# The third weight slot split ahead of the norm's root in four stages, and the first state-space weights split in the stage ahead

## The reference, cut to what matters

```
def rmsnorm(x, g):
    xf = x.astype(jnp.float32)
    y = xf * lax.rsqrt(jnp.mean(xf * xf, axis=-1, keepdims=True) + EPS)
    return (y * g.astype(jnp.float32)).astype(x.dtype)
...
        h = rmsnorm(x, norm_mix[i])
        proj = h @ w_in[i]
...
        merged = (jax.nn.sigmoid(gate_a) * (attn @ w_attn_branch[i])
                  + jax.nn.sigmoid(gate_b) * (ssd @ w_ssd_branch[i]))
        x = x + merged @ w_out[i]
        h = rmsnorm(x, norm_cross[i])
        x = x + cross_attention(h, rmsnorm(mem, norm_mem[i]), w_xq[i], w_xkv[i], w_xo[i])
        h = rmsnorm(x, norm_ffn[i])
        x = x + jnp.square(jax.nn.relu(h @ w_up[i])) @ w_down[i]
```

## Time and profile before

| | |
|---|---|
| median of 3 runs | 2428.04 us (2426.35 to 2433.3) |
| span of the profiled execution, first to last instruction | 2430.9 us |
| busy share of the span | PE 92%, DVE 58%, ACT 44%, POOL 14% |
| mean granted TensorE clock | 0.960 |

### The profile page before, as it was taken

One profiled execution on the slowest core, in us unless ns is written; L12 is line 12 of the kernel. 1 busy time (PEld: TensorE's weight loads), 2 busy tenths in 40 slices (PEclk: granted clock), 3 DMA queues, 4 the chain that ended last, 5 costly groups with the idle time before them and its releaser, 6 DMA issues.

```text
span 2430.9 us, 32383 instructions
## 1 busy us (share of the span) xinstructions
PE 2235.2 (92%) x11925; PEld 1869.3 (77%) x11925; DVE 1404.1 (58%) x2174; ACT 1081.8 (44%) x1863; POOL 345.0 (14%) x431
## 2 busy tenths in 40 slices
PE   6999989999997999889999999999989998969997
PEld 5888768888886787668888888987778886757774
DVE  4657435777776565553443435758646656456665
ACT  4445534666665423442322323654333344245553
POOL 1000001112111000000000000853334440012001
PEclk8999999999998999999999999999989999969999
DMA  5222422232221613223223143131010014259995
GB/s 193 86 76 32 96 90 65 59 90 61 74 60 56 234 44 104 76 97 104 87 88 103 35 157 104 36 109 66 27 44 1 1 39 170 109 203 395 415 414 196
DMA packets 169179, 273.23 MB, mean 112 GB/s; under 512 B 9865, under 2 KB 142297, under 8 KB 159193
## 3 DMA queue, kind: packets, MB, share of 16 engines
q1 hardware_dynamic: 164585, 255.22, 31.0%
q0 software_dynamic: 4464, 16.25, 1.8%
HBM read 240.00 MB, written 31.46 MB: 112 GB/s over the span
## 4 chain that ended last, share of the span: by engine, by line
PE 78%; DVE 8%; ACT 7%; DVEq 3%; issue 2%; DMA 1%; POOL 1%; POOLq 1%; ACTq 0%; SPq 0%
PE ps L178 19%; PE ps L179 18%; PE ps L180 18%; PE ps L3630 3%; ACT pair L364 1%; PE ps L3040 1%; DVE pair L370 1%; PE ps L3057 1%; PE ps L1119 1%; PE ps L1661 1%; PE ps L3594 1%; PE ps L1637 1%; PE ps L3008 1%; PE ps L2638 1%; PE ps L1097 1%
## 5 line engine op out<-in xcount | busy, mean ns | idle before, releaser
L180 PE MATMUL ps<-pair,pair 128*128 128x512 f32 (+1 forms) x2216 | 804.5, 363 | 0.0
L178 PE MATMUL ps<-pair,pair 128*128 128x512 f32 (+1 forms) x1960 | 731.7, 373 | 48.5 <-DVE pair L370 14.5
L179 PE MATMUL ps<-pair,pair 128*128 128x512 f32 (+1 forms) x1960 | 732.2, 374 | 0.0
L180 PEld LDWEIGHTS ps<-pair,pair 128*128 128x128 f32 x2216 | 422.4, 191 | 68.9
L178 PEld LDWEIGHTS ps<-pair,pair 128*128 128x128 f32 x1960 | 374.4, 191 | 113.7 <-issue 34.2
L179 PEld LDWEIGHTS ps<-pair,pair 128*128 128x128 f32 x1960 | 375.5, 192 | 68.1 <-issue 7.2
L370 DVE TENSOR_TENSOR pair<-ring,pair 128x2048 fp32r<-128x2048 f32 x95 | 219.0, 2305 | 139.0 <-ACT pair L364 138.8
L364 ACT ACTIVATE pair<-ring 128x2048 fp32r<-128x2048 f32 x102 | 194.6, 1908 | 202.5 <-PE ps L180 194.1
L880 DVE TENSOR_TENSOR arena<-ps,arena 128x512 f32<-128x512 f32 x56 | 38.7, 690 | 137.8 <-PE ps L180 137.8
L178 PE MATMUL ps<-part,pair 128*128 128x512 f32 x256 | 104.1, 407 | 11.8 <-DVE part L423 6.1
L1842 DVE SCALAR_TENSOR_TENSOR arena<-arena 128x512 f32<-128x512 f32 x128 | 97.8, 764 | 25.1 <-issue 12.1
(11 more groups left out here) (551 smaller groups left out, 3788.8 us busy)
## 6 DMA issues: line engine op xcount, KB each, us to landing
ring<-in_w_in SPq DMA_DIRECT2D x54, 1024.0 KB, 6.5
arena<-in_w_exp_down SPq DMA_DIRECT2D x23, 1024.0 KB, 10.9
ring<-in_w_up SPq DMA_DIRECT2D x16, 1024.0 KB, 5.4
ring<-in_w_down SPq DMA_DIRECT2D x16, 1024.0 KB, 5.1
ring<-in_w_exp_gate SPq DMA_DIRECT2D x16, 1024.0 KB, 8.9
ring<-in_w_exp_up SPq DMA_DIRECT2D x16, 1024.0 KB, 10.9
expert_results<-arena SPq DMA_DIRECT2D x22, 512.0 KB, 11.3
ring<-in_w_in SPq DMA_DIRECT2D x16, 512.0 KB, 6.0
```

What stands on the lines that cost most here:

```text
L178: nc.tensor.matmul(out, lhs[1], rhs[0], start=start, stop=False)
L179: nc.tensor.matmul(out, lhs[0], rhs[1], start=False, stop=False)
L180: return nc.tensor.matmul(out, lhs[0], rhs[0], start=False, stop=stop)
```

## The change

`third_early` is set in the four stages that begin with a norm. There the split of slot 2 moves out of `put(0)` into the lead: on ACT behind the squares and ahead of the root (with its wait for PE's end of slot 0), on DVE ahead of the variance. In the second block this puts it ahead of both roots.

In the attention branch's stage the steps beside it get fixed places and a sixth one is added: it splits the first two column chunks of the state-space weights. ACT waits there until 4 of the 8 parked chunks have landed, and SP waits for the same before it issues the fifth. In the state-space stage's first group those two splits are gone, and two SiLUs stand ahead of the fourth `copy_up`.

```diff
@@ Project.put @@
-        if k + 2 < self.n or self.repeat > 1:
+        if k == 0 and self.third_early:
+            pass
+        elif k + 2 < self.n or self.repeat > 1:
@@ Project @@
+    def third_hi(self, act):
+        act.wait_ge(self.core.unit_ready, self.unit0 + self.plan[0]["j"].per_slot)
+        self.split_hi(act, 2, 0)
@@ Project.scalar, Project.vector @@
+        if self.third_early:
+            self.lead["act"](act, self.third_hi)
+        elif "act" in self.lead:
...
+        if self.third_early:
+            self.lead["dve"](dve, lambda dve: self.split_lo(dve, 2, 0))
+        elif "dve" in self.lead:
@@ TokenScale @@
             act.activation(self.sq[:, c, :], self.src[:, c, :], ACT.Square).then_inc(squares, 1)
+        between(act)
         act.wait_ge(var_ready, self.n_var + 1)
...
         dve.tensor_tensor(sq[:, 0, :], sq[:, 0, :], sq[:, 1, :], ALU.add).then_inc(squares, 1)
+        between(dve)
         dve.wait_ge(summed, self.n_summed + 1)
@@ stages_ssd @@
+            PARKED_FIRST = DC // 2
             def decay_vector(dve, step):
+                if step == 5:
+                    for n in range(2):
+                        first_weights["lo"](dve, n)
             def decay_scalar(act, step):
+                if step == 5:
+                    act.wait_ge(s_unparked, 16 * PARKED_FIRST)
+                    for n in range(2):
+                        first_weights["hi"](act, n)
...
-                             beside=Beside(5, pe=decay_tensor, act=decay_scalar, dve=decay_vector))
+                             beside=Beside(6, at=(1, 22, 30, 40, 50, 57), pe=decay_tensor, act=decay_scalar,
+                                           dve=decay_vector))
...
                     sp.wait_ge(core.unit_stored["dve"], dve0 + m + 1)
+                    if m == PARKED_FIRST:
+                        sp.wait_ge(s_unparked, 16 * PARKED_FIRST)
                     sp.dma_start(parked[:, m, :], merged[:, m, :]).then_inc(s_unparked, 16)
...
+            def first_weights_hi(act, n):
+                src, hi, _ = weights_of(n)
+                if n == 0:
+                    act.wait_ge(w_landed0, 48)
+                act.activation(hi, src, ACT.Copy).then_inc(w_hi, 1)
+
+            def first_weights_lo(dve, n):
+                src, hi, lo = weights_of(n)
+                dve.wait_ge(w_hi, n + 1)
+                dve.tensor_tensor(lo, src, hi.bitcast(F32), ALU.subtract).then_inc(w_split, 1)
@@ ssd_scalar, first @@
                     act.wait_ge(s_unparked, 16 * DC)
-                    weights_hi(0, 0)
-                    weights_hi(0, 1)
                     for n in range(4):
+                        if n == 3:
+                            silus(0, (0, 1))
                         copy_up(0, n)
                         next_weights(0, n)
-                    silus(0, (0, 1, 2))
+                    silus(0, (2,))
@@ ssd_vector, first @@
                     dve.memset(up, 0.0).then_inc(pads_zeroed, 1)
-                    weights_lo(0, 0)
-                    weights_lo(0, 1)
```

More of the change, by code:

```diff
@@ L252, in __init__ @@
         self.next, self.ahead, self.source_ahead, self.begun = None, 0, False, 0
+        self.third_early = False
         assert core.top <= core.weights_at, core.top
@@ L522, in scalar @@
                 self.source_hi(act, k, 0)
-        if "act" in self.lead:
+        if self.third_early:
+            self.lead["act"](act, self.third_hi)
+        elif "act" in self.lead:
             self.lead["act"](act)
@@ L604, in __init__, with scalar @@
         self.n_squares, self.n_summed, self.n_var, self.n_root = core.norm_counts(DC + 1, 2, 2, 1)
-    def scalar(self, act):
+    def scalar(self, act, between):
         squares, summed, var_ready, root_ready = self.core.norm_sems
@@ L626, in tensor, with vector @@
                                   start=True, stop=True).then_inc(summed, 1)
-    def vector(self, dve):
+    def vector(self, dve, between):
         core = self.core
@@ L1057, in stage_attention @@
                                           dve=lambda dve, step: normed1.vector(dve, step - 2)))
+            first["project"].third_early = True
             normed1.begin()
@@ L1346, in decay_vector @@
                                       rounded[turn_hi][0:2 * H, :].bitcast(F32), ALU.subtract).then_inc(s_a_ready, 1)
+            first_weights = {}
             def decay_scalar(act, step):
+                if step == 5:
+                    act.wait_ge(s_unparked, 16 * PARKED_FIRST)
+                    for n in range(2):
+                        first_weights["hi"](act, n)
                 if step == 0:
@@ L1677, in ssd_tensor @@
                 looped(pe, first, middle, last)
+            def first_weights_hi(act, n):
[7 more added lines that the diff above has]
+                dve.tensor_tensor(lo, src, hi.bitcast(F32), ALU.subtract).then_inc(w_split, 1)
+            first_weights.update(hi=first_weights_hi, lo=first_weights_lo)
             def ssd_scalar(act):
@@ L2104, in stages_cross @@
             queries["project"].begun = DC - 1
+            queries["project"].third_early = True
             yield queries
@@ L2208, in rows_in, with lead_vector @@
                 return lambda i, r: w_down[n][:, :, i * 256:(i + 1) * 256]
-            def lead_vector(dve):
-                root.vector(dve)
+            def lead_vector(dve, between):
+                root.vector(dve, between)
                 dve.tensor_tensor(two_gains, col["norm_final"], col["norm1_g_2"], ALU.mult)
@@ L2221, in stages_ffn @@
             ffn["project"].begun = DC - 1
+            ffn["project"].third_early = True
             yield ffn
```

1 line of the change is left out of this document (removed).

## The result

The changed kernel took 2410.89 us (median of 5 runs, 2405.38 to 2417.32) beside 2429.83 for the kernel before (5 runs). The ratio is 0.9917, with a 95% interval of 0.9891 to 0.9944. So it is faster, by 0.65 to 0.83%.

What follows compares the result with a forecast made beforehand. It took PE's work, waits and half clock as the bound. Gains of 2.7 + 8.0 + 0.35 - 3.8 + 13.0 = 20.3 us off the median of 2428.04 gave 2407.7, range 2402 to 2415.

Steps and rivals of the forecast that it cites:

- Stage one, -2.7: Stage one: slot 2's 6.37 us wait goes, slot 4's grows to about 5; the stores' chain lets 2.7 us be gained.
- Feed-forward, -8.0: Feed-forward stage: slot 2's wait of 5.70 us and 2.3 of half clock go, slot 3's split being just in time.
- the second rival: Feed-forward: slot 3 becomes late where slot 2 was, with a wait of 3.3 us and the sum 2411; chance 0.10.
- Second block, +3.8: Second block's first projection: the early split delays roots and diagonal, costing a 2.3 us wait plus 1.5 of half clock.
- Branch and state space, -13.0: Branch to first state-space group: 3.45 + 4.35 + 2.25 + 2.9 us gained from waits and half clock; bounds 3.45 and 13.3.
- Step 1: Beside the branch: PE's step 1 moves from piece 13 to piece 22 and its 3.45 us wait goes.
- The start: Start of the state-space stage: PE waits 1.64 us instead of 5.99, gaining 4.35, and stays at full clock, gaining 2.25.
- The SiLUs: State space's first group: with two SiLUs ahead of the fourth copy, PE goes on to z 2.9 us earlier.
- The margin of 3.2: Branch's end: the early lo parts finish at 347.2, 3.2 us before DVE's last store could follow at 350.4.
- slower: Branch's end: the wait for four parks holds the last store and all engines, if parks land over 23.5 us later; chance 0.03.
- The weights split ahead: State-space start: rival that the early splits don't start the stage, the old wait remains and the whole is 2414.4; chance 0.13.
- The clock goes the other way: Whole kernel: half clock appears behind no new wait and also goes from another, giving 2402 to 2404 us; chance 0.06.

Runs made afterwards that it cites:

- e9: e8's kernel with stage one's nine normed-pair steps at pieces 72 to 136 instead of 40 to 104; 2402.02 us, ratio 0.9881 to the kernel before.
- e7: The changed kernel run again as it is, one run; 2409.45 us.
- e3: The changed kernel with the branch's part undone, leaving only the early split of slot 2 in four stages; 2426.67 us, ratio 0.9971 to the kernel before.
- e11: The changed kernel as it is, timed again on one chip beside the kernel before and e12; 2411.90 us, ratio 0.9935.
- e8: The changed kernel with the second block's slot 2 split put behind both roots and the diagonal; 2408.57 us, ratio 0.9906 to the kernel before.
- e2: The changed kernel without the early split of slot 2 in any stage, leaving only the branch's part; 2417.17 us, ratio 0.9949 to the kernel before.
- e4: The kernel before with only the branch's five steps moved, to pieces 1, 22, 30, 40 and 50; one run, 2437.51 us beside 2430.72.
- e10: The changed kernel with ACT and SP waiting for seven parked chunks instead of four; one run, 2411.11 us.
- e12: The changed kernel with both e8's and e9's edits, timed beside e11; 2401.85 us, ratio 0.9887 to the kernel before.

## Why the prediction was right, by its own steps

The forecast of 2407.7 lies 3.2 us below the measured median and inside its range; the difference to the kernel before, 20.3, was measured as 20.2 and 15.8 by the ratios of the two timings. The sum is right partly because errors cancel: the branch gave more than I said and the second block's wait cost less, the feed-forward stage of the profile gave less, and the stages ahead of the last stretch add up to 22.5 us in the profile (27.3 less 4.8), more than either timing shows. That the median came out within 3.2 us is therefore in part luck. Point by point:

- **Stage one, -2.7: right, with its reason.** 2.65 measured, and the wait at slot 4 grew by 2.85, as said (2.8). The prediction didn't name the 2.07 at slot 3, but its reason (the stores' chain sets the pace and moves only by what is taken out) covers it. e9 took 1.9 more out of the chain ahead of slot 4 and PE's wait there fell by 1.9; e7 lost 1.55 on PE and lost nothing.
- **Feed-forward, -8.0: right.** 8.3 in e3, e7 and e11 (360.80, 360.85, 360.83 against 369.07). The changed profile's 6.9 has no wait more; it is a slower pace at a granted clock of 1.00 (0.2333 us from one matmul's start to the next in the middle of the stage, and 0.2324 in the others; the 0.2318 and 0.2310 written for e7 were too low). Slot 3's split was ready just in time, at 1063.7, so the second rival didn't come about.
- **Cross attention, -0.35:** 0.5 measured, too small to tell.
- **Second block, +3.8: the direction and the wait right, the half clock wrong.** The wait is 1.98 (2.3 predicted), the diagonal ends 4.70 after the variance as said, and e8 shows the cause. The step that failed is "whether half clock follows: I take 1.5, by the nearest row": no run has it, and the term is 1.6 to 2.5 (of the whole, 3.8). The row of 2.08 us chosen as the nearest was a wait of nearly the same length at slot 4 of stage one; 1.5 was lost there and nothing here.
- **Branch and state space, -13.0: too small.** 14.65 in the changed profile, in e2 and (with the half clock at 299.4) in e11, and 16.3 in e7 without that. Step 1 was put at 3.45 and is worth 5.2 (e4): I counted the wait and forgot that the twelve small matmuls behind it ran at half clock; 1.6 of it went again, in the profiles with half clock near the branch's start. The start was put at 4.35 and is 5.0, since PE waits 0.98 and not 1.64. The SiLUs are 2.8 in wait, as said, and 1.4 in half clock, which I had left out.
- **The margin of 3.2: wrong by 2.4.** It is 0.8, in two profiles (0.77 and 0.72, in e7) and by e10's price. In the changed profile PE ends the branch within 0.2 us of where I said (the 1.7 more from step 1 and the half clock cancel); the two hi and two lo parts take 3.46 (3.7 said). It is the fourth parked chunk: it landed 4.25 ahead of DVE's last store (343.13 and 347.38), where my numbers had 7.1 (343.5, and 354.05 less 3.45), so 2.85 later. Most of that is a misread row. The 8.4 us that I added to 338.29 belong to the first chunk; the fourth was issued at 342.06, took 6.65 and landed at 348.7, not by 347: 1.75. The other 1.1 came with the change: the chunk is issued 0.2 nearer to the store and takes 7.5 and not 6.65 to land. In the eight profiles in which SP holds the fifth chunk back until the fourth has landed, the fourth takes 7.5 to 8.0 us; in the four without that (before, e3, e4, and e10, which holds the eighth) 6.65 to 6.83. The wait on SP, of which I said that it delays only parks 5 to 8, thus goes with a later fourth; why isn't known. The rival "slower" had this mechanism and its place; its price, as e10 shows, starts at 0.8 us and not 3.2.
- **The rivals.** The weights split ahead do start the stage (0.98 us). "The clock goes the other way" came half true: half clock is missing behind the second block's wait and appears at 299.7 without any new wait. The Trainium skill (TensorE: Matmul & The Clock Gate, "What's actually happening") says the position of these changes varies from run to run. By that sentence the trace agrees: the wait ahead of the branch is 2.48 us in all twelve profiles, and five of them (the changed kernel, e2, e9, e11, e12) have 7 or 8 matmuls at half clock that begin within 1.6 us behind it, while seven have none; of the three profiles of the changed kernel itself two have them (the branch takes 50.2) and one hasn't (48.6).

## What to carry to other kernels

A wait removed is worth what the engine behind it can do before it meets the next late thing: read the waiting engine's list, take out what you moved, and see which producer is then late (6.4 us of wait gave 2.65 here, and moving unrelated steps of the producers took another 3.6 off its waits). Moving work ahead of a norm's root is free only where the engine would have idled there; where it has to wait for a slot to be released first, the root waits too, and the better place is behind the diagonal. A margin is read from the row of the very transfer that is waited for, not from the longest of its group: that cost 1.75 of my 3.2. Two profiles of one kernel differ by 5.5 us in the stretch behind the second block's first projection, so compare by stage, with a second profile of the changed kernel, before a difference is explained.

## What the runs showed of the hardware that I had not expected

- Half clock behind a wait falls on small matmuls too: the twelve 128x128 matmuls of step 1 take 1.25 to 1.26 us without a wait and about 2.6 behind 3.45 us (before at a granted clock of 0.50, and e4). In e3, with the same wait, 7 of the products behind them are at half clock as well, and the branch takes 60.13 and not 58.75.
- A wait of 2 to 3 us may or may not bring half clock, with the same code and the same wait: none behind 1.98 at the second block's spread in any of six profiles, 8 matmuls behind 2.07 at slot 3 in one of nine (e7), 7 or 8 behind 2.48 ahead of the branch in five of twelve, and 8 behind 3.0 at slot 4 in e12 but none in e9. Ahead of the branch it costs 1.6 to 1.8 us each time.
- Half clock costs nothing where PE meets a wait for other engines afterwards (e7: 1.55 lost, the wait 1.55 shorter).
- The spread between runs goes with the granted clock: the changed kernel's five runs have 0.968, 0.967, 0.966, 0.960, 0.962 at 2405.4, 2406.8, 2410.9, 2417.3, 2415.3 us.
- At a granted clock of 1.00 the pace of the feed-forward stage still has two values, 360.8 and 362.15 us for its 1546 or 1547 recorded matmuls. What sets it is open.
- Eight transfers of 256 KB to HBM, issued behind 3.1 MB of weights, took 8.3 to 8.6 us to land for the first and 2.0 for the last, which is issued when the others have landed (all twelve profiles).
